# Expert blocks: four bank reads placed before the second copy of the next rows, and the next block's bias and first products issued bank by bank

## The reference

```python
    order = jnp.argsort(flat_e)
    ...
    xs = xf[row_tok].reshape(n_blocks, MOE_BLOCK, D)

    def expert_block(args):
        xb, e = args
        hu = xb @ w_up[e] + b_up[e]
        x_glu = jnp.minimum(hu[:, :D_FF], SWIGLU_LIMIT)
        x_lin = jnp.clip(hu[:, D_FF:], -SWIGLU_LIMIT, SWIGLU_LIMIT)
        act = x_glu * jax.nn.sigmoid(SWIGLU_ALPHA * x_glu) * (x_lin + 1.0)
        return act @ w_down[e] + b_down[e]
```

## Time and profile before

| | |
|---|---|
| median of 3 runs | 2753.83 us |
| lowest, highest | 2746.51, 2763.89 us |
| the profiled execution | 2755.39 us |
| its span, first to last instruction | 2754.2 us |
| mean granted clock of TensorE | 0.948 |
| TensorE busy | 2543.1 us, 92% |
| VectorE, ScalarE, GpSimd busy | 36%, 20%, 8% |
| read from HBM | 537.24 MB |

### The profile page before, as it was taken

The page is one execution under the profiler, slowest core; times in us unless marked ns, Lnnn a source line. Parts: engine busy times, 40 slices in busy tenths (PEclk is TensorE's granted clock), DMA queues, the critical chain, the costliest instruction groups (busy, mean ns, idle before and its releaser), DMA issues. The chain is left out here.

```text
span 2754.2 us, 27360 instructions
## 1 busy us (share of the span) xinstructions
PE 2543.1 (92%) x10309; PEld 1239.8 (45%) x10309; DVE 980.7 (36%) x2130; ACT 562.6 (20%) x1298; POOL 217.4 (8%) x387
## 2 busy tenths in 40 slices
PE   5988999969999999999999997999899789999998
PEld 2544676533343333443433432655444444454453
DVE  2666453542212111212111211624466764342272
ACT  1255431100000000000000001311455552200250
POOL 1000442020010101010100000200000000000000
PEclk8989999969999999999999998999889899999889
DMA  9101578259999999779589999320000002112000
GB/s 339 66 31 62 196 272 324 114 221 369 407 416 419 415 416 416 290 265 400 201 332 417 415 420 393 128 88 31 0 1 1 1 1 84 46 64 89 31 1 31
DMA packets 146590, 565.46 MB, mean 205 GB/s; under 512 B 18278, under 2 KB 39199, under 8 KB 108435
## 3 DMA queue, kind: packets, MB, share of 16 engines
q1 hardware_dynamic: 127336, 515.97, 47.5%
q0 software_dynamic: 16224, 42.52, 4.1%
q10 hardware_dynamic: 2890, 5.13, 0.5%
HBM read 537.24 MB, written 26.35 MB: 205 GB/s over the span
## 5 line engine op out<-in xcount | busy, mean ns | idle before, releaser
L1807 PE MATMUL ps<-ring,mem 128*32 128x512 f32 (+2 forms) x1888 | 520.6, 607 | 13.6 <-issue 13.6
L217 PE MATMUL ps<-mem,ring 128*128 128x512 f32 (+1 forms) x1056 | 423.2, 561 | 2.6 <-DVE mem L761 1.6
L217 PE MATMUL ps<-ring,mem 128*128 128x512 f32 (+5 forms) x1136 | 388.2, 498 | 18.2 <-ACT ring L2493 8.5
L1807 PEld LDWEIGHTS ps<-ring,mem 128*32 128x32 f32 (+2 forms) x1888 | 190.7, 147 | 279.8 <-issue 279.8
L217 PEld LDWEIGHTS ps<-mem,ring 128*128 128x128 f32 x1056 | 201.8, 192 | 214.0 <-issue 205.2
L217 PEld LDWEIGHTS ps<-ring,mem 128*128 128x128 f32 x1136 | 198.6, 194 | 192.5 <-issue 159.3
L1836 PE MATMUL ps<-ring,mem 128*32 128x512 f32 (+2 forms) x1056 | 273.5, 618 | 10.7 <-issue 10.7
L223 PE MATMUL ps<-mem 128*128 128x128 f32 (+3 forms) x1203 | 194.2, 294 | 56.0 <-DVE mem L2633 11.7
L1807 PE MATMUL ps<-mem 128*32 128x512 f32 (+2 forms) x800 | 234.9, 596 | 2.6 <-issue 2.6
L223 PEld LDWEIGHTS ps<-mem 128*128 128x128 f32 (+3 forms) x1203 | 145.0, 147 | 183.4 <-issue 115.8
L1868 DVE COPY mem<-ps 128x512 f32<-128x512 f32 x48 | 33.3, 693 | 504.8 <-PE ps L223 504.8
(11 more groups left out here) (377 smaller groups left out, 2332.9 us busy)
## 6 DMA issues: line engine op xcount, KB each, us to landing
ring<-in_w_up SPq DMA_DIRECT2D x91, 2048.0 KB, 16.7
ring<-in_w_down SPq DMA_DIRECT2D x47, 2048.0 KB, 22.8
mem<-in_w_up SPq DMA_DIRECT2D x37, 2048.0 KB, 19.2
mem<-in_w_down SPq DMA_DIRECT2D x17, 2048.0 KB, 22.3
ring<-in_w_ada SPq DMA_DIRECT2D x12, 2048.0 KB, 8.2
ring<-in_mod_w SPq DMA_DIRECT2D x8, 2048.0 KB, 10.2
ring<-in_cd_w_in SPq DMA_DIRECT2D x6, 2048.0 KB, 7.7
y_rows<-mem POOLq DMA_DIRECT2D x23, 512.0 KB
```

The source lines that it names most:

```text
L217: i = e.matmul(o, l, r, start=(start and n == 0), stop=(stop and n == len(pairs) - 1))
L1807: m = e.matmul(PS[n][c0:c0 + rows, :], XGT[:, u, k * 128 + c0:k * 128 + c0 + rows], wt[:, kk, n * 512:n * 512 + 512], start=False, stop=(k ...
```

## The change

It has two parts. On VectorE the second copy of the next block's rows moves from ahead of `dve_swiglu` to behind its four bank reads (`between`). On TensorE the wait for all four banks at the start of `pe_up` is split into one for each bank; each stands directly in front of the bank's bias product. For that, the bias product of a bank moves to directly in front of the bank's first product, and for `q` = 0 the bank is the outer loop: bias, product k = 0, product k = 1 for bank 0, then the same for banks 1, 2 and 3. The bias products now also stand behind the wait for the first weights and for the first half of the rows. For `q` = 1 to 3 the order stays. The number of instructions is the same.

```diff
-        if i:
-            e.wait_ge(L.glu, 2 * i)
-            e.wait_ge(L.lin, 2 * i)
-        for n in range(4):
-            for c0, rows, x in [(c, r, x) for c0, rows, x, tile in parts for c, r in tiles(c0, rows)]:
-                bias_product(e, PS[n], x, n, 0, c0, rows)
         for q in range(4):
             wts = []
             for c0, rows, x, tile in parts:
                 wt, ready = tile(q)
                 e.wait_ge(*ready)
-                wts += [(c, r, wt.rearrange("p (k n) -> p k n", n=2048)) for c, r in tiles(c0, rows)]
+                wts += [(c, r, x, wt.rearrange("p (k n) -> p k n", n=2048)) for c, r in tiles(c0, rows)]
             e.wait_ge(L.x_copied, 2 * i + q // 2 + 1)
-            for kk in range(2):
+
+            steps = [(kk, n) for n in range(4) for kk in range(2)] if q == 0 else [(kk, n) for kk in range(2) for n in range(4)]
+            for kk, n in steps:
                 k = 2 * q + kk
-                for n in range(4):
-                    for c0, rows, wt in wts:
-                        m = e.matmul(PS[n][c0:c0 + rows, :], XGT[:, u, k * 128 + c0:k * 128 + c0 + rows], wt[:, kk, n * 512:n * 512 + 512],
-                                     start=False, stop=(k == 7))
+                if k == 0:
+                    if i:
+                        e.wait_ge(L.glu if n < 2 else L.lin, 2 * i - 1 + n % 2)
+                    for c0, rows, x, wt in wts:
+                        bias_product(e, PS[n], x, n, 0, c0, rows)
+                for c0, rows, x, wt in wts:
+                    m = e.matmul(PS[n][c0:c0 + rows, :], XGT[:, u, k * 128 + c0:k * 128 + c0 + rows], wt[:, kk, n * 512:n * 512 + 512],
+                                 start=False, stop=(k == 7))
             m.then_inc(L.up, 1)
             between(q)
...
-    def dve_swiglu(e, L, i):
+    def dve_swiglu(e, L, i, between=None):
...
             e.tensor_scalar(T2[:, c], PS[2 + n], 7.0, -7.0, ALU.min, ALU.max).then_inc(L.lin, 1)
+        if between:
+            between()
         e.wait_ge(L.lin, 2 * (i + 1))
...
                 dve_copy_x(e, main, i + 1, 0)
-                dve_copy_x(e, main, i + 1, 1)
-            dve_swiglu(e, main, i)
+            dve_swiglu(e, main, i, (lambda: dve_copy_x(e, main, i + 1, 1)) if i + 1 < NMAIN else None)
```

## The result

| | before | changed |
|---|---|---|
| median, 18 runs each | 2754.07 us | 2766.94 us |
| lowest, highest | 2746.51, 2764.12 us | 2759.94, 2775.33 us |
| ratio to before | | 1.0037, interval 1.0026 to 1.0048 |
| the profiled execution's span | 2754.2 us | 2761.7 us |
| mean granted clock of TensorE | 0.948 | 0.955 |

The changed kernel is slower, by 10.2 us (7 to 13) by the ratio on 2754, less than 1%. The two medians lie 12.9 us apart. Single runs of one kernel scatter by more than this difference, 17.6 us before; only the many runs together tell the two kernels apart.

What follows compares the result with a forecast made beforehand. Transfers bound the kernel where full, TensorE where they have holes. Stretches summed -1.5 (passed on to transfers), +2, +6.7 and 0, taken as +8.7 on 2755.39; against the median 2762.5 us, range 2746 to 2774.

Steps and rivals of the forecast that it cites:

- A: Block 0 to 1, at 624 us, two up steps in direct succession: wait and clock together gain 4.6 us.
- B: At 1265 us, up following up after a pair of blocks sharing weights: wait and clock gain 5.5 us.
- C: At 1448 us, up following up after a pair sharing weights: gain 5.5 us, taken to fall into slack.
- First stretch: 590 to 640 us: two blocks pay 2 x 1.53, less a gain of 4.6, making -1.5 us.
- Long stretch: 640 to 1062 us, transfers full: nine up steps add 13.8 against 13.0 us of slack; taken as +2 us.
- Third stretch: 1062 to 1420 us, TensorE sets the end: eight up steps at 1.53 less a gain of 5.5, +6.7 us.
- Last stretch: 1420 to 1710 us, transfers full: five up steps' 7.7 us fall into 17.8 us of slack, 0.
- 1: Bias products, all blocks: a group costs only 0.23 us, giving 2750.6 us; chance 0.18.
- 2: Bias products, all blocks: they cost nothing, so the total is -10.1 us, 2743.7 us; chance 0.05.
- 3: All expert blocks: no slack, slots come back late everywhere, +21.1 us, 2774.9 us; chance 0.12.
- 4: Where up follows up: TensorE still idles long enough for the clock to fall, 4.5 us lost, 2767; chance 0.04.
- 5: Around lone bias products: neighbours lose hidden weight loads; slower by over 1%, 2782 us at 0.9 a group; chance 0.03.

Runs made afterwards that it cites:

- the kernel with bias products behind: The changed kernel with each bank's first product starting the accumulation and the four bias products together behind the q = 0 products, all blocks: 2745.23 us, ratio 0.996.
- the kernel with blocks 2 to 10 alone: The kernel before with the bias products apart, bank by bank, in blocks 2 to 10 only: ratio 1.0021, +5.8 us.
- the kernel with blocks 19 to 23: The kernel before with the bias products apart, bank by bank, in blocks 19 to 23 only: ratio 1.0008, +2.2 us.
- the kernel with bias products behind and the full wait: The changed kernel with bias products together behind q = 0, VectorE's old order and TensorE waiting for all four banks: 2758.29 us, ratio 0.9995.
- the kernel with three blocks apart: The changed kernel with bias products and waits bank by bank only in blocks 1, 15 and 19, the other 21 keeping them together: 2752.02 us, ratio 0.9986.

## Why the prediction was right, point by point

**Gain 1, the wait.** Predicted 0.43 us of idle at A; measured 0.44 there, 0.30 and 0.32 at B and C.

**Gain 2, the clock.** Predicted to stay up; it did at all three. With the loss taken off, A gave 4.5 (a shift from +3.69 to +0.60, and 1.4 us of bias products in it), B 5.7 and C 6.1, against 4.6 and twice 5.5. That B came out so near is in part luck: what the low clock costs differs from trace to trace. In the five other kernels that keep the wait of 3.27 us, the step behind B took only 1.6 to 1.7 us more than an undisturbed one, not 2.7. That the gain is real and a sum on its own, the kernel with bias products behind shows: -11.0 for a predicted 10.1.

**The price of a group.** Taken as 0.51 from groups of two and four, with 0.23 and zero as bounds. Measured 0.51 in blocks of kind S and D. In P and Q, where a bank's bias is two or four narrower products, three more groups cost 1.43 and 1.35 us a block in place of 1.53. The lower bound, 0.23 from the two clocks, came out as the price of a lone product without the switch, 0.21.

**First stretch.** Predicted -1.5, measured -1.9.

**Long stretch.** This is the term that was mis-sized. Predicted +3.5 from 656 to 1069 us (-1.5 to +2), measured 7.03 - 0.60 = +6.4. I had named the mechanism, slots given back late, and its measure, +6 for half of the slack lost, and then took a value nearer to the best case without a row for it. Of the 2.9 us that were missed, 1.7 are another thing, a new fall of the clock behind the last of these waits; the wait, then the window of the step behind it:

```profile
1067.59 0.72 PE L1807 MATMUL ps<-ring,mem 128*64 128x512 f32 x1 [2.58 <-issue]
...
1067.60:1076.30 8.70, 8.70 (x32) 3.12 (x33) 0.00 (x0) 0.00 (x0) 0.00 (x0) 0.80 1.03 411
```

Before, this wait was 0.72 us and the step took 7.02; now it is 2.58 and 8.71, at a granted clock of 0.80. In the kernel with blocks 2 to 10 alone the wait is 2.41 us long and the step 7.02, and its loss over the stretch is 5.0. So late slots cost about 5 us (6.4 - 1.7 = 4.7 and 5.0), the clock the rest. Of 13.0 us of slack 13.2 - 6.4 = 6.8 are used in the changed kernel and 13.2 - 5.0 = 8.2 with these blocks alone.

**Third stretch.** Predicted +6.7, measured 13.32 - 7.03 = +6.3.

**Last stretch.** Predicted 0, measured 12.72 - 13.32 = -0.6. C's gain (6.1) and the five blocks' loss (7.3) nearly cancel, and what is left vanishes in waits for weights; that the loss alone vanishes too, the kernel with blocks 19 to 23 shows. But those waits fell from 17.8 to 13.1, where I had written that they stay near 18.

**The sum.** Predicted +8.7, measured +10.2 by the ratio and by the trace. It is nearer than its worst term, since that one was 2.9 too low and the three others together 1.4 too high; that part is luck.

**Rivals.** 1 and 2 fall with the price of 0.51; 3 falls with the run of blocks 19 to 23; 4 with the clock at A and B; 5 with the price, though what it names, weight loads beside a lone bias product that are no longer hidden, does occur and is part of the 0.51.

## What to carry to other kernels

Products that use a strip of the array are cheap side by side and dear alone: splitting a group of four to make its waits finer cost about 1.4 to 1.5 us a block in all 24 blocks, to shorten a wait that existed in three. When a wait is to be split by bank, leave the small products together and move them to where all banks are free anyway; an accumulation can be started by the first large product instead. And slack that stands at the end of a stretch with full transfers is worth less than it looks to work added ahead of it, here a half to two thirds, if that work holds back the slots.

## What the runs showed of the hardware

- A switch of TensorE from full-height products to a strip of three rows and back costs 0.30 us: a lone group measured 0.51, 0.21 of it streaming. Groups of two and four strips cost the same 0.51 and 0.5 by the sums on the rows before. Beside the strip neither weight load overlaps with a product.
- The clock behind an idle of TensorE at A, B and C: at 0.30 to 0.44 us and at 1.47 us it stayed up in all three places each, at 2.1 to 2.2 us it fell in two of three, and at 3.27 us in all eighteen (three places in each of the six kernels that keep that wait). There the step took 1.5 to 3.1 us longer than an undisturbed one. The length of the idle alone doesn't decide it: behind waits for weights, 1.91 us (at 742 us, in the kernel with bias products behind and the full wait) lost the clock, with a step of 8.70 us at a granted 0.80, and 3.39 us (at 967 us, in the kernel with three blocks apart) didn't, with a step of 7.01 at 1.00. That the same kernel can lose or keep some 2 to 3 us at such a place from one execution to the next is a likely part of why the runs of one kernel scatter over 17 us, but each kernel has one trace and it was not tested.
